# Address remainders of the fp32r row tiles, interleaved input loads, and shifted side steps in a two-block transformer kernel

## The chip, the cores and the metric

The kernel runs on one core of one Trainium2 chip. The metric is the device time of one execution in microseconds (us), and smaller is better. Engines are named as in the profile: PE (TensorE matmul), PEld (its weight loads), DVE (VectorE), ACT (ScalarE), POOL (GpSimd) and SP (SyncE), which here only issues DMAs.

## The reference

Two blocks run one after the other on x of 256 rows by 2048 features, all in fp32. What the kernel must compute, cut to its matrix products:

```
block 1: proj = rms_norm(x) @ w_in       (queries, keys, values of 3 attentions; 12 gate units)
         o1..o3 = nsa / sliding-window / moba attention, nsa also over compressed keys (cmp_w1)
         merged = sum_m sigmoid(gate_m) * (o_m @ w_branch[m]);   x += merged @ w_out
         x += relu(norm(x) @ w_mlp_in)^2 @ w_mlp_out;            x = norm(x)
block 2: proj2 = norm(x) @ w_in_2;  pool mixer and HGRN2 mixer;  x += mixed @ w_out_2
         x += cross_attention(norm(x), norm(mem)) (xattn_wq, wk, wv, wo)
         x += mixture of 16 experts (two per row), routed by norm(x);  out = norm(x)
```

## The kernel before, in words

**Weights and rows.** Up to the experts every large product is one form. SP streams weight tiles of 1 MB (two pieces of 128x1024 fp32) into the ring `RAW` of 8 pieces (`stream_load`, L199 to L218; the wait at L208 is for a free place, the plan is `make_plan`, L2165). `split` (L249 to L259) turns a piece into two fp32r halves: ACT copies it to `HI` (L257), DVE subtracts that from the piece into `LO` (L259); HI and LO have four places. `Stage.gemm` (L274) takes pieces in order. One piece is one **block**: 2 slices of the contraction x 2 halves of the rows x the three products of L301 (xh·wh), L302 (xh·wl) and L303 (xl·wh), so 12 matmuls of 128x512. The rows x are the stationary operand, 128 columns (512 bytes) of one slot; the weight piece is the moving operand. `split` is called three blocks ahead (`LEAD`), at the start of each block. After block j the function `hooks[j]` is called, and it writes its instructions into the queues at that point. That is how all other work is put beside the products: each engine works through its own queue in program order, so a waiting instruction holds all behind it on its engine.

**Where the rows lie.** The rows are kept as XH and XL, 32 slots of 128x256 fp32r each. Slots 0 to 15 are in the tensors XH and XL, which are allocated first (L117); slots 16 to 31 are in XH2 and XL2 (L128), allocated after the small tensors; RAW, HI, LO and WORK follow (L130 to L133). A partition holds 16,384 bytes of each of XH, XL, X, Y, then IDENT 512, SWH and SWL 1,536 each, GATE 192, GAIN 384, SMALL 2,048, FULL 4 (places are multiples of 32). From XH to XH2 this is 71,776 bytes, 140 x 512 + 96. XH2, XL2, RAW, HI and LO are 16,384 or 32,768 bytes long, so all of them, WORK, and later WIDE, XS and ROUNDED, start on the same remainder modulo 512, which is 96 above that of XH, XL, X, Y and IDENT.

**Which slots each stage reads** (`kt0` of `gemm`), in blocks: w_in 88 lower; 12 gate units 96 lower; cmp_w1 16 (upper slots, but 30 stationary columns and 256 moving); w_branch 16 lower and 32 upper; w_out 32 lower; the MLP 128 upper (first product) and 128 lower (second); w_in_2 80 upper; xattn_wkv, beside which HGRN runs, 64 lower; w_out_2 32 upper; xattn_wq 32 lower; xattn_wo 32 upper. That is 456 blocks on the lower slots, 304 on the upper and 16 small ones, 776 in all.

**PSUM.** A gemm accumulates in one pair of banks. It waits until the pair's last result was read (`ev[pair]`, L290): by `store` (L473; two ACT copies, L479, then a DMA) or by `add_to_x` (L483; a DVE add, L486).

**Side work the change touches.**
- Start (L523 to L579): four loads of x on SP (L527), then the weight stream; IDENT and GAIN on ACT. `first_T(c)` transposes chunk c of x (L325) and splits it (ACT L338, DVE L342). Chunks 0 and 1 come ahead of the first gemm, 2 and 3 in hooks 1 and 3. Blocks 2c and 2c+1 need chunk c.
- First gate unit (L693): `gate_weights` in hook 0 (ACT L666, DVE L668); `compress_in` (L632; PE L637 waits for a load of stored projections, L626) in hooks 1 and 4; `gate_logits` (48 small matmuls in two parts, which wait for L668) in hooks 3 and 5; `gate_values` in 7.
- Gate units 0 to 9 of L1011 all use pair 0. In units 0 to 7 runs one attention step each (`attend`, L860): transposes after block 0, `logits` after 1 (its DVE chain ends at L914), `exps(0)` after 3 and `exps(1)` after 4 (ACT, L916), `probs` after 5 (DVE, L941 to L956), `probs_T` after 6 (PE L965), `values` after 7 in banks 2 and 3, pair 1. `wide_load` is in hook 2.
- `project_add` (L1080), for w_out and w_out_2: four gemms on pairs 1, 0, 1, 0. What follows it starts on pair 0. Ahead of the w_out_2 one, the last store is of pair 1.
- HGRN (L1318 to L1493, twice): 32 blocks with steps in hooks. `exps_of(0)` after block 4; level n has its DVE work (L1415 `masked`, L1367 `exponents`, L1387 `factors`) in hook 6+2n and its matmuls (`products`, L1412) in hook 7+2n; the output steps are in hooks 25, 26, 27, 28 and 30.
- Routing, beside the last xattn_wo stage (L1682 to L1729): for chunks 0 to 2 `routed_T` (transposes, squares on ACT, `token_hi` on ACT) in hook 2c+2 and `chunk_router` (router matmuls, and `token_lo`, a DVE subtraction, L1680) in hook 2c+3; then the transposes and sums of chunk 3, the routing itself, and `token_lo(3)`.

**Experts** (from L1748): 192 MB of weights go into the ring WIDE of 24 pieces; SP waits for PE to free pieces (L236).

Of the kernel before, what the change touches and what calls it, by code (L numbers as in the profile page):

```python
# [100 lines left out]
def build(nc, a, out):  # L101
    ctx = ExitStack()
    with ctx:
        def sb(name, shape, dt=F32):
            return ctx.enter_context(nc.sbuf_tensor(name, shape, dt))
# [10 lines left out]

        lower = [sb(n, [P, DK, S], F32R) for n in ("XH", "XL")]  # L117
# [8 lines left out]
        FULL = sb("FULL", [P, 1], I32)  # L126
        upper_memory = ctx.enter_context(ExitStack())
# [71 lines left out]
        def stream_load(plan):  # L199

            b = 0
            for passes, tiles in plan:
                def body(it, base, n=2 * len(tiles)):
                    for k, (w, index) in enumerate(tiles):
                        first = base + 2 * k
                        slot = first % RAW_SLOTS

                        sp.wait_ge(lo_done, it * n + (first + 2))  # L208
                        src = w[bass.ds(index(it), 1)].rearrange("t p n -> p (t n)")
                        sp.dma_start(RAW[:, slot:slot + 2, :].rearrange("p s n -> p (s n)"), src).then_inc(raw_in[slot // 2], 16)  # L210
                assert 2 * len(tiles) % RAW_SLOTS == 0
                if passes == 1:
                    body(0, b)
                else:
                    with nc.Fori(0, passes, engines=[ENG.SP]) as it:
                        body(it, b)
                b += passes * 2 * len(tiles)
            assert b == experts  # L218
# [303 lines left out]

        small_load([a["w_in_gates"]], 24)  # L523
        x_in = [ctx.enter_context(nc.semaphore(f"x_in{c}")) for c in range(4)]
        for c in range(4):
            t = slice(c * 512, (c + 1) * 512)
            sp.dma_start(X[:, :, t], a["x"][0].rearrange("(h p) n -> p h n", p=P)[:, :, t]).then_inc(x_in[c], 16)  # L527
        dve.sem_inc(lo_done, RAW_SLOTS)
        pe.sem_inc(pe_done, HL_SLOTS)
        stream_load(plan[:-2])  # L530
        ld[2].inc(act.dma_start(IDENT[:, :], a["ident"]), 16)
        ld[2].inc(act.dma_start(GAIN[:, :, :].rearrange("p g k -> p (g k)"), a["gains"]), 16)
# [36 lines left out]

        for b in range(LEAD):  # L570
            if b < 2:
                first_T(b)
            split(b)
# [4 lines left out]
        hooks1 = {1: lambda: first_T(2), 3: lambda: first_T(3), 5: sums_of_input, 6: bias_table}  # L578
# [104 lines left out]
        def gate_values():  # L683
# [5 lines left out]
            for h in range(NH):  # L689
# [3 lines left out]
        s = gate_unit(0, {0: gate_weights, 1: lambda: compress_in(0), 3: lambda: gate_logits(0), 4: lambda: compress_in(1),  # L693
                          5: lambda: gate_logits(DK // 2), 7: gate_values})
# [165 lines left out]
        def attend(n):  # L860
# [142 lines left out]
            hooks = {0: [transposes], 1: [logits], 3: [lambda: exps(0)], 4: [lambda: exps(1)], 5: [probs], 6: [probs_T], 7: [values]}  # L1003
# [7 lines left out]
        for n in range(10):  # L1011
# [7 lines left out]
            if 2 <= n < 7:  # L1019
                hk.setdefault(2, [])  # L1020
                if n in (2, 4, 5, 6):
                    hk[2].append(lambda k={2: 0, 4: 1, 5: 2, 6: 3}[n]: wide_load(k))
            if finish:
                hk[0] = [finish] + hk.get(0, [])
            gate_unit(0, both(hk)).end()
# [54 lines left out]
        def project_add(kt0, ready, hooks, to, gain):  # L1080
# [9 lines left out]
            for c in range(4):  # L1090
# [3 lines left out]
                pair = (1, 0, 1, 0)[c]  # L1094
# [223 lines left out]
        for g in range(2):  # L1318
# [156 lines left out]
            for n in range(len(levels)):  # L1475
                k = 6 + 2 * n
# [5 lines left out]
            last = 7 + 2 * len(levels)  # L1482
# [199 lines left out]
        def routed_T(c):  # L1682

            rows_T_of_x(c)
            column_sums(c, squares=SQUARES)
            token_hi(c)

        def chunk_router(c):

            router_part(c)  # L1690
            token_lo(c)
# [26 lines left out]
        rows_T_of_x(3)  # L1718
        column_sums(3, squares=SQUARES)
# [564 lines left out]
```

## Time and profile before

| what | us |
|---|---|
| median of 3 runs | 2929.2 (2928.99 to 2929.81) |
| the profiled execution | 2927.93 |
| its span in the trace | 2926.4 |
| PE busy in the span | 2796.6 (96%) |
| DVE busy / ACT busy | 1468.2 / 1189.0 |
| DMA, MB moved | 672.70, mean 230 GB/s |

The profile gives each group of instructions by line. In a timeline row the columns are the start in us, the duration in us, engine, line, operation, the tiles (out <- in) with shapes, and the count; a bracket gives the idle time of the engine just before and what ended it. Matmuls are pipelined, so the distance between starts, not the duration, is what a matmul takes.

### The profile page before, as it was taken

The page shows a single profiled execution, that of the slowest core. Times are in us where ns is not written, and L with a number is a line of the kernel's source. Part 1 is how long each engine was busy: PE and PEld are TensorE (multiplying, and loading weights), DVE is VectorE, ACT ScalarE, POOL GpSimd, SP SyncE. Part 2 cuts the span into 40 slices and gives each one's busy share as a digit, 9 for nine tenths or more (in the row PEclk, how much of TensorE's full clock was granted, in tenths as well). Part 3 has the DMA queues.
Part 4 walks back from the last instruction along what each step waited for, and adds up shares of the span by engine and source line. Part 5 has one row for each costly group of instructions (what it writes and reads, how often), then busy time and mean ns, then how long its engine had stood idle before and what let it go on. Part 6 is the DMA issues. An engine that isn't in the chain of part 4 may idle for free.

```text
span 2926.4 us, 33379 instructions
## 1 busy us (share of the span) xinstructions
PE 2796.6 (96%) x12846; PEld 2098.3 (72%) x12846; DVE 1468.2 (50%) x1673; ACT 1189.0 (41%) x1536; POOL 12.9 (0%) x20
## 2 busy tenths in 40 slices
PE   8999999999999999999999999999999998989896
PEld 6887877777887888888887788787888774433332
DVE  4444555546655555555555744577654463312122
ACT  4443545544344444444444644545444341000001
POOL 0000000000000000000000000000000000000000
PEclk9999999999999999999999999999999998999999
DMA  7765644556646555555555475545455448999997
GB/s 276 278 210 200 245 155 155 180 177 230 225 174 221 195 186 186 186 186 185 187 174 185 166 281 207 204 150 187 170 190 184 156 161 334 419 420 419 420 419 311
DMA packets 115648, 672.70 MB, mean 230 GB/s; under 512 B 12061, under 2 KB 17613, under 8 KB 40656
## 3 DMA queue, kind: packets, MB, share of 16 engines
q1 hardware_dynamic: 85696, 612.41, 56.8%
q10 hardware_dynamic: 27552, 46.69, 4.5%
q0 software_dynamic: 2288, 12.08, 1.2%
q8 instruction: 74, 1.21, 0.2%
q14 instruction: 38, 0.31, 0.0%
HBM read 647.51 MB, written 28.35 MB: 231 GB/s over the span
## 4 chain that ended last, share of the span: by engine, by line
PE 81%; DMA 8%; ACT 4%; DVE 4%; issue 1%; DVEq 1%; ACTq 0%; SPq 0%; PEldq 0%; PEld 0%
PE PS L301 22%; PE PS L302 22%; PE PS L303 22%; PE PS L1955 6%; DMA WIDE<-in_w_up 4%; DMA WIDE<-in_w_gate 2%; DMA WIDE<-in_w_down 2%; ACT HI L257 1%; DVE LO L259 1%; PE PS L325 1%; PE PS L1893 1%; PE PS L1412 1%; ACT Y L922 1%; PE PS L2052 1%; PE PS L896 0%
## 5 line engine op out<-in xcount | busy, mean ns | idle before, releaser
L259 DVE TENSOR_TENSOR LO<-RAW,HI 128x1024 fp32r<-128x1024 f32 x776 | 941.9, 1223 | 873.2 <-ACT HI L257 868.3
L301 PE MATMUL PS<-HI,XH 128*128 128x512 f32 (+1 forms) x3104 | 1233.4, 397 | 20.5 <-DVE LO L259 7.6
L302 PE MATMUL PS<-LO,XH 128*128 128x512 f32 (+1 forms) x3104 | 1216.5, 392 | 0.0
L303 PE MATMUL PS<-HI,XL 128*128 128x512 f32 (+1 forms) x3104 | 1214.2, 391 | 0.0
L257 ACT ACTIVATE HI<-RAW 128x1024 fp32r<-128x1024 f32 x776 | 813.4, 1058 | 851.1 <-PE PS L303 774.5
L301 PEld LDWEIGHTS PS<-HI,XH 128*128 128x128 f32 (+1 forms) x3104 | 579.2, 187 | 158.5 <-issue 12.9
L303 PEld LDWEIGHTS PS<-HI,XL 128*128 128x128 f32 (+1 forms) x3104 | 578.9, 186 | 131.2
L302 PEld LDWEIGHTS PS<-LO,XH 128*128 128x128 f32 (+1 forms) x3104 | 579.4, 187 | 129.1 <-issue 2.9
L1955 PE MATMUL PS<-WIDE,XS 128*64 128x512 f32 x1024 | 229.6, 596 | 27.7 <-DMA WIDE<-in_w_up 18.4
L1955 PEld LDWEIGHTS PS<-WIDE,XS 128*64 128x64 f32 x1024 | 75.4, 137 | 166.1 <-issue 165.7
L1955 PE MATMUL PS<-WIDE,Y 128*64 128x512 f32 x512 | 116.7, 598 | 9.3 <-ACT Y L2009 5.5
L486 DVE TENSOR_TENSOR X<-PS,X 128x1024 f32<-128x1024 f32 x88 | 107.6, 1222 | 27.8 <-PE PS L303 27.8
L1955 PEld LDWEIGHTS PS<-WIDE,Y 128*64 128x64 f32 x512 | 36.4, 136 | 75.0 <-issue 67.7
L2021 DVE SCALAR_TENSOR_TENSOR ROUNDED<-PS,SMALL,ROUNDED 128x512 fp32r<-128x512 f32 x32 | 24.0, 751 | 113.9 <-ACT ROUNDED L2020 113.9
L2020 ACT ACTIVATE ROUNDED<-PS,SMALL 128x512 fp32r<-128x512 f32 x32 | 22.0, 687 | 127.8 <-PE PS L1955 127.8
L479 ACT ACTIVATE WORK<-PS,SMALL 128x512 f32<-128x512 f32 x82 | 51.8, 683 | 40.2 <-PE PS L303 38.9
L2003 DVE TENSOR_TENSOR Y<-Y,PS 128x512 f32<-128x512 f32 x8 | 5.5, 686 | 116.0 <-PE PS L1955 116.0
L2009 ACT ACTIVATE Y<-PS 128x512 f32<-128x512 f32 x8 | 4.8, 597 | 133.2 <-PE PS L2007 133.2
L1937 ACT ACTIVATE ROUNDED<-PS 128x256 fp32r<-128x256 f32 x8 | 3.1, 383 | 136.2 <-PE PS L1932 136.2
L332 ACT ACTIVATE XH<-PS 128x512 fp32r<-128x512 f32 x60 | 32.7, 594 | 60.1 <-PE PS L325 60.1
L334 DVE TENSOR_TENSOR XL<-PS,XH 128x512 fp32r<-128x512 f32 x60 | 38.7, 686 | 31.9 <-ACT XH L332 31.9
L1998 DVE TENSOR_TENSOR Y<-Y,PS 128x512 f32<-128x512 f32 x8 | 5.5, 687 | 94.8 <-ACT Y L1996 94.8
(348 smaller groups left out, 1357.0 us busy)
## 6 DMA issues: line engine op xcount, KB each, us to landing
RAW<-in_w_in SPq DMA_DIRECT2D x132, 1024.0 KB, 4.9
RAW<-in_w_mlp_in SPq DMA_DIRECT2D x64, 1024.0 KB, 4.8
RAW<-in_w_mlp_out SPq DMA_DIRECT2D x64, 1024.0 KB, 4.8
WIDE<-in_w_gate SPq DMA_DIRECT2D x64, 1024.0 KB, 23.6
WIDE<-in_w_up SPq DMA_DIRECT2D x64, 1024.0 KB, 19.7
WIDE<-in_w_down SPq DMA_DIRECT2D x64, 1024.0 KB, 22.2
RAW<-in_w_out SPq DMA_DIRECT2D x32, 1024.0 KB, 4.9
RAW<-in_xattn_wkv SPq DMA_DIRECT2D x32, 1024.0 KB, 4.8
```

The source lines that it names most:

```text
L257: act.activation(r["hi"][:, hl, :], r["raw"](k), ACT.Copy).then_inc(hi_done, 1)
L259: dve.tensor_tensor(r["lo"][:, hl, :], r["raw"](k), r["hi"][:, hl, :].bitcast(F32), ALU.subtract).then_inc(lo_done, 1)
L301: pe.matmul(o, xh, wh, start=kt == 0, stop=False)
L302: pe.matmul(o, xh, wl, start=False, stop=False)
L303: mm = pe.matmul(o, xl, wh, start=False, stop=kt == kn - 1)
L325: mm = pe.transpose(PS[:, i, q * S + h * P:q * S + h * P + P], src[:, h, (j + q) * P:(j + q + 1) * P], IDENT[:, :])
L332: hi = s_hi.inc(act.activation(dh, PS[:, i, :], ACT.Copy))
L334: lo = s_lo.inc(dve.tensor_tensor(dl, PS[:, i, :], dh.bitcast(F32), ALU.subtract))
L479: ins = act.activation(STAGE[:, slot, h * W512:(h + 1) * W512], PS[:, 2 * pair + h, :], func, scale=r[:, h:h + 1])
L486: return ev[pair].h, ev[pair].inc(dve.tensor_tensor(X[:, :, cols], pair_ap(pair), X[:, :, cols], ALU.add))
L922: act.activation(v, v, ACT.Exp, bias=NM[:, c:c + 1], accum_out=RS[:, c:c + 1])
L1955: mm = pe.matmul(PS[x * HALF:(x + 1) * HALF, bank, :], lhs(q, x), w[x][:, q, :], start=first and q == 0, stop=last and q == 3)
```

## The change

It adds two unused SBUF tensors: `shift_rows`, 96 bytes per partition, ahead of XH, and `shift_upper`, 416 bytes, between FULL and XH2. XH to Y and the small tensors move up by 96 bytes, all from XH2 on by 512. From XH to XH2 it is then 72,192 bytes, 141 x 512. The loads of x go between the first four weight tiles on SP. Hooks, pairs and the place of `token_lo` change as in the diff.

```diff
+        sb("shift_rows", [P, 24])
         lower = [sb(n, [P, DK, S], F32R) for n in ("XH", "XL")]
...
         FULL = sb("FULL", [P, 1], I32)
+        sb("shift_upper", [P, 104])
...
-        def stream_load(plan):
+        def stream_load(plan, beside):
...
                         slot = first % RAW_SLOTS
+                        if isinstance(first, int) and first < RAW_SLOTS:
+                            beside(k)
...
+        ld[2].inc(act.dma_start(IDENT[:, :], a["ident"]), 16)
+        ld[2].inc(act.dma_start(GAIN[:, :, :].rearrange("p g k -> p (g k)"), a["gains"]), 16)
         small_load([a["w_in_gates"]], 24)
...
-        for c in range(4):
+        dve.sem_inc(lo_done, RAW_SLOTS)
+        pe.sem_inc(pe_done, HL_SLOTS)
+        def input_rows(c):
             t = slice(c * 512, (c + 1) * 512)
             sp.dma_start(X[:, :, t], a["x"][0].rearrange("(h p) n -> p h n", p=P)[:, :, t]).then_inc(x_in[c], 16)
-        dve.sem_inc(lo_done, RAW_SLOTS)
-        pe.sem_inc(pe_done, HL_SLOTS)
-        stream_load(plan[:-2])
-        ld[2].inc(act.dma_start(IDENT[:, :], a["ident"]), 16)
-        ld[2].inc(act.dma_start(GAIN[:, :, :].rearrange("p g k -> p (g k)"), a["gains"]), 16)
+        stream_load(plan[:-2], input_rows)
...
+        first_T(0)
         for b in range(LEAD):
-            if b < 2:
-                first_T(b)
             split(b)
...
-        hooks1 = {1: lambda: first_T(2), 3: lambda: first_T(3), 5: sums_of_input, 6: bias_table}
+        hooks1 = {0: lambda: first_T(1), 2: lambda: first_T(2), 4: lambda: first_T(3), 5: sums_of_input, 6: bias_table}
...
-        s = gate_unit(0, {0: gate_weights, 1: lambda: compress_in(0), 3: lambda: gate_logits(0), 4: lambda: compress_in(1),
-                          5: lambda: gate_logits(DK // 2), 7: gate_values})
+        s = gate_unit(0, {0: gate_weights, 1: lambda: gate_logits(0), 2: lambda: gate_logits(DK // 2), 3: lambda: compress_in(0),
+                          4: gate_values, 5: lambda: compress_in(1)})
...
-            hooks = {0: [transposes], 1: [logits], 3: [lambda: exps(0)], 4: [lambda: exps(1)], 5: [probs], 6: [probs_T], 7: [values]}
+            hooks = {0: [transposes], 1: [logits], 2: [lambda: exps(0)], 3: [lambda: exps(1)], 4: [probs], 6: [probs_T], 7: [values]}
...
-                    hk[2].append(lambda k={2: 0, 4: 1, 5: 2, 6: 3}[n]: wide_load(k))
+                    hk[2].insert(0, lambda k={2: 0, 4: 1, 5: 2, 6: 3}[n]: wide_load(k))
...
-            gate_unit(0, both(hk)).end()
+            gate_unit(n // 9, both(hk)).end()
...
-                pair = (1, 0, 1, 0)[c]
+                pair = c % 2
...
-                k = 6 + 2 * n
+                k = 7 + 2 * n
...
-            last = 7 + 2 * len(levels)
+            last = 8 + 2 * len(levels)
...
             rows_T_of_x(c)
+            if c:
+                token_lo(c - 1)
             column_sums(c, squares=SQUARES)
...
             router_part(c)
-            token_lo(c)
...
         rows_T_of_x(3)
+        token_lo(2)
         column_sums(3, squares=SQUARES)
```

## Rows read from the trace of the kernel before

**Rows 1.** The page: busy time by engine, and the group of one DVE line.

```profile
PE 2796.6 (96%) x12846; PEld 2098.3 (72%) x12846; DVE 1468.2 (50%) x1673; ACT 1189.0 (41%) x1536; POOL 12.9 (0%) x20
...
L259 DVE TENSOR_TENSOR LO<-RAW,HI 128x1024 fp32r<-128x1024 f32 x776 | 941.9, 1223 | 873.2 <-ACT HI L257 868.3
```

**Rows 2.** Windows view: stretch, length, busy (count) by engine, PE clock, DMA share, GB/s.

```profile
2440.00:2450.00 10.00, 9.48 (x51) 6.24 (x51) 3.32 (x8) 1.67 (x2) 0.00 (x0) 0.88 0.31 125
...
2600.00:2900.00 300.00, 263.01 (x1225) 106.96 (x1222) 61.98 (x107) 24.28 (x48) 0.00 (x0) 1.00 1.01 420
```

**Rows 3.** PE's waits: who waited for whom, us in total, times, longest.

```profile
PE PS L965 <- DVE Y L956: 10.3, 8, 2.5
...
PE PS L1412 <- DVE Y L1394: 8.3, 4, 3.3
...
PE PS L301 <- ACT WORK L479: 5.7, 4, 1.4
...
PE PS L301 <- DVE X L486: 2.8, 2, 1.4
```

**Rows 4.** PE's timeline on lower slots (w_in): first and last of 85 starts.

```profile
60.16 0.40 PE L303 MATMUL PS<-HI,XL 128*128 128x512 f32 x1
...
79.76 0.40 PE L303 MATMUL PS<-HI,XL 128*128 128x512 f32 x1
```

**Rows 5.** PE's timeline on upper slots (w_in_2): first and last of 88 starts.

```profile
1700.20 0.39 PE L303 MATMUL PS<-HI,XL 128*128 128x512 f32 x1
...
1719.92 0.39 PE L303 MATMUL PS<-HI,XL 128*128 128x512 f32 x1
```

**Rows 6.** PE's timeline in the experts: 64 stationary columns, from XS and from Y.

```profile
2456.82 3.65 PE L1955 MATMUL PS<-WIDE,XS 128*64 128x512 f32 x16
...
2464.55 13.95 PE L1955 MATMUL PS<-WIDE,XS 128*64 128x512 f32 x64
...
2493.52 3.65 PE L1955 MATMUL PS<-WIDE,Y 128*64 128x512 f32 x16
```

**Rows 7.** Timeline of the start, all engines.

```profile
9.28 1.57 ACT L338 ACTIVATE XH<-PS,GAIN 128x256 fp32r<-128x256 f32 x4
...
14.44 1.06 ACT L257 ACTIVATE HI<-RAW 128x1024 fp32r<-128x1024 f32 x1 [3.59 <-DMA RAW<-in_w_in]
...
16.80 0.80 PE L301 MATMUL PS<-HI,XH 128*128 128x512 f32 x1 [3.58 <-DVE LO L259]
```

**Rows 8.** PE's timeline: second stage's start, first stop on a pair.

```profile
46.28 0.50 PE L301 MATMUL PS<-HI,XH 128*128 128x512 f32 x1 [1.36 <-ACT WORK L479]
```

**Rows 9.** Timeline of the first gate unit, all engines.

```profile
280.76 0.55 DVE L668 TENSOR_TENSOR SWL<-WORK,SWH 128x384 fp32r<-128x384 f32 x1
...
280.98 1.12 PE L637 MATMUL PS<-IDENT,Y 128*128 128x128 f32 x4 [4.82 <-DMA Y<-proj]
```

**Rows 10.** DVE's timeline in attention step 5.

```profile
537.55 0.16 DVE L914 TENSOR_SCALAR SMALL<-SMALL 128x8 f32<-128x8 f32 x1
...
544.59 1.23 DVE L259 TENSOR_TENSOR LO<-RAW,HI 128x1024 fp32r<-128x1024 f32 x1 [2.06 <-ACT HI L257]
...
547.11 1.22 DVE L956 TENSOR_TENSOR Y<-Y,SMALL 128x1024 f32<-128x1024 f32 x1
```

**Rows 11.** PE's timeline in HGRN's first pass: its stops.

```profile
1894.35 2.05 PE L1412 MATMUL PS<-Y 128*128 128x128 f32 x16 [3.31 <-DVE Y L1394]
...
1902.83 2.05 PE L1412 MATMUL PS<-Y 128*128 128x128 f32 x16 [0.83 <-DVE Y L1394]
...
1978.73 1.09 PE L325 MATMUL PS<-IDENT,WORK 128*128 128x128 f32 x8 [0.71 <-DVEq L1463]
```

**Rows 12.** Timeline of the routing: PE and DVE.

```profile
2406.08 1.09 PE L325 MATMUL PS<-IDENT,X 128*128 128x128 f32 x8 [2.18 <-DVE X L486]
...
2419.01 1.23 DVE L1680 TENSOR_TENSOR XL<-X,XH 128x1024 fp32r<-128x1024 f32 x1 [2.45 <-ACT XH L1674]
...
2421.42 1.51 PE L325 MATMUL PS<-IDENT,X 128*128 128x128 f32 x8 [2.28 <-DVE X L486]
```

## The prediction

> **What bounds the kernel now.** I read the page first: PE is busy for 96% of the span and DVE for half of it [rows 1], so up to the experts PE's own pace and its stops make the time. The windows come next, to see where that ends. In the experts DMA is busy throughout (share 1.01, 420 GB/s), while just before them its share is 0.31 [rows 2]: SP waits for PE to free the first pieces. So the experts, 201 MB at that rate or 480 us, go by DMA, but they begin when PE gets there, and what PE gains before that moves the end one for one. What it gains inside the experts is hidden by DMA.
>
> Third, PE's timeline, for the distance between starts. On lower slots 84 distances take 19.60 us, 0.2333 us each [rows 4]; on upper slots 87 take 19.72, 0.2267 each [rows 5]. The lines, shapes, HI and LO are the same, so the slot alone differs: 6.7 ns, or 2.9%. Fourth, PE's waits: some 27 us of stops in four groups that the change touches, the largest on DVE's probabilities [rows 3].
>
> **The remainder.** 456 blocks x 12 = 5472 matmuls read lower slots, and 304 x 12 = 3648 upper ones. Today HI, LO and the upper slots share a remainder, and the lower ones start 96 bytes below it; afterwards all are alike, as the upper ones are today. The trace has no lower slot at that remainder, so the cost is bounded: nothing gained, or all of 5472 x 6.67 ns = **36.5 us**. I take all. The reason: a slot's second half lies 512 bytes after its first, XL 16,384 after XH, LO as far after HI, and none of these steps shows in the distances, so the address matters, if at all, modulo 512; the other explanation, that the tensor lies far away, has to skip all these steps and act only between two tensors. Against it: with 64 stationary columns, 16 matmuls from Y, which is off the remainder, take 3.65 us as 16 from XS, which is on it [rows 6]. But there the distance is (13.95 - 3.65) / 48 = 0.215, so the load, half as long, may be no limit. Two rules of the Trainium skill speak against this part. "TensorE: Matmul & The Clock Gate", section "Back-to-back issue gap", lets the distance depend on the moving columns alone. "SBUF — State Buffer", section "Specifications (TRN2)", counts in lines of 16 bytes, of which 96 is a multiple. By either, this term would be 0; rows 4 against 5 differ all the same, and the rule is the first rival below.
>
> What becomes of the faster pace where PE waits for a chain of ACT and DVE is subtracted in each part. DVE, ACT and DMA operations keep their number and shape. The longest DVE one takes 1.22 us of a block of 12 x 0.2333 = 2.8 [rows 1, 4], so the split keeps up at 2.72.
>
> **The start.** Four loads of x (2 MB) stand ahead of the first weights. ACT has split chunk 0 at 9.28 + 1.57 = 10.85 and then waits for the weights until 14.44; PE's products begin at 16.80 [rows 7]. Afterwards 0.5 MB of x stand ahead of the 1 MB tile, half of what lands before it today, so it is there before 10.85, and all moves by 3.6. But chunk 1's eight transposes used to lie in that gap. Now they stand after block 0 in PE's way: 1.09 us for eight [rows 12], double that at the 1.2 GHz level. Net **-2.6 us**, between 0 and -3.6. The later x loads are needed two blocks apart, 5.6 us, against 1.5 MB; SP's queue issues the same eight DMAs.
>
> **First gate unit.** PE stops 4.82 us before `compress_in` for a load and goes on at 280.98 [rows 9]. The move takes this wait out of the way, since the load lands long before hook 3. But `gate_logits` now comes in hook 1, and it needs L668, which ends at 280.76 + 0.55 = 281.31 [rows 9], because ACT issues seven DMAs before the split and the gate weights. So another wait takes its place, 0.4 longer, and the two blocks ahead of it end 0.16 earlier against a fixed chain. **+0.5 us**; the bounds are -4.8 (if L668 gets done in time) and +2 (if `compress_in(1)`, now two blocks before the end, holds back the compress gemms).
>
> **Attention.** Eight stops before `probs_T`, 10.3 us [rows 3]. In step 5 the maxima are ready at 537.7 (L914), DVE splits a piece from 544.59 and the probabilities end at 548.33 (L956) [rows 10]. Now ACT waits for the maxima in hook 2 with one split (an ACT copy of 1.06 us [rows 7]) behind it instead of in front, then runs both `exps` with one split between. By my count along its queue that lets the last LO start at 543.6 instead of 544.6; the probabilities end 1.0 earlier, and PE, by now 0.4 ahead, still waits 0.4. In steps 0 and 2, `compressed_T` no longer stands between the maxima and the second exponentials, and the stop of 2.5 goes entirely. ACT's splits behind the wait have three blocks of lead, which covers them; without that cover each would cost PE 1 us. Left over I put 1.4 us, so **-8.9**; bounds -3 and -10.3. `wide_load`, put ahead of `exps(0)`, issues its three DMAs before the wait, as before.
>
> **Pairs.** PE waits for a pair to be read four times on L479, 5.7 us, and twice on L486, 2.8 [rows 3]. The first of the four, 1.36 at 46.28 [rows 8], stays. The others go: after gate units 8 and 9, around both `project_add`. Unit 9 writes banks 2 and 3, which step 7 has left by then. (5.7 - 1.36) + 2.8: **-7.1 us**. Bounds 0 and -7.1; the other pair was read a stage before.
>
> **HGRN.** Per pass PE stops 3.31 and 0.83 before `products` and 0.71 before the output transposes [rows 11]. One block more of cover is worth 2.8, but DVE's queue takes one more LO of 1.22 [rows 1] ahead of level 0's factors: 3.31 + 1.2 - 2.8 = 1.7. The second stop grows, since ACT's store of the first quarter now waits behind level 1's exponential: about 1.2. So 4.1 becomes 2.9. The chain is DVE's, and PE arrives 0.8 earlier with its faster blocks: 3.7. The output chain keeps its distance of blocks, which are 0.4 shorter in sum: 0.71 becomes 1.1. Per pass -0.4 and +0.4: **0**; bounds -3 and +2.
>
> **Routing.** PE stops 2.18 and 2.28 for L486, both times behind a `token_lo` (L1680, 1.23 us) that stands before it on DVE [rows 12]. The first loses 1.1. The second `token_lo` also waited for ACT until 2419.01, so that stop goes entirely, -2.3. In its new place the subtraction delays the last column sums by 1.2; I take them to have 0.5 of room beside the router's products (an estimate, no row here), so 0.7 comes back. **-2.7 us**; bounds 0 and -4. This chain is PE's start of the experts, so it counts in full.
>
> **The sum.** 36.5 + 2.6 - 0.5 + 8.9 + 7.1 + 0 + 2.7 = **57.3 us**. Against the profiled execution, 2927.9 (its span is 2926.4), that gives 2870.6. It stands 1.3 below the median of 2929.2; on the median, **2871.9**.
>
> **Rivals.** (1) Place, not remainder, sets the 6.7 ns. For it: rows 6 show no effect of the remainder, and the skill's rules above. Then the other terms alone remain: 2929.2 - 20.8 = **2908.4**, somewhat less since the faster pace no longer eats into gains. Chance 0.08. (2) The stops only move: a wait for the maxima at the head of ACT's queue delays splits until PE waits for LO, as in the gate unit one wait replaces another. For it: ACT and DVE are in order, and HGRN's chain is DVE's own. Against: three blocks of lead. The pace alone: 2929.2 - 36.5 = **2892.7**. Chance 0.05. (3) Slower: 512 bytes up is a worse place, and each of the 9120 matmuls loses one more such step of 6.7 ns. That costs 60.8 against 20.8 gained: **2969.2**; it decides from 2.3 ns on. Only the fact that the cause of the step is unseen speaks for it. Chance 0.02.
>
> **How the numbers follow.** The forecast has 0.85. Its own terms, with the bounds that can coincide, give -11 (the gate wait gone, no wait left in attention, HGRN at its best) and +14 (half of attention, start and routing missing, HGRN slower): 2861 to 2886. That holds some 0.83, and the other cases stay outside. Within 0.2% (5.9 us, about what a measurement of this kernel tells from no change) lies almost nothing, 0.01; slower is rival 3 with a little for an unseen wait, 0.03; faster 0.96.
>
> **What would show it.** In the profile of the changed kernel: lower-slot distances of 0.2267 (0.2333 is rival 1, over 0.2333 rival 3); the first product near 13.2; PE still stopped for 5 us in the first gate unit, now at `gate_logits` behind L668; the waits on L956 near 1.4 in sum; two waits on L479 and L486 together at most; 3.7 per pass on L1412; one stop of about 1 us in the routing. More than 3 us of PE waiting for L259 would be rival 2.

## The result, and the profile after

The changed kernel takes 2880.5 us (median of 4 runs, 2876.7 to 2882.3) against 2929.4 (2929.0 to 2929.8) for the kernel before, measured beside it: ratio 0.983, 95% interval 0.981 to 0.985. That is 48.8 us less (46.8 between the two profiled executions, 2927.9 and 2881.1). The forecast was 2871.9, 57 less, with a range of 2861 to 2886. So the direction and the range held, and 9 us of the gain are missing.

The page of the changed kernel, whose profiled execution took 2881.1 us with a span of 2879.6:

```profile
PE 2761.4 (96%) x12846; PEld 2097.8 (73%) x12846; DVE 1466.3 (51%) x1673; ACT 1186.0 (41%) x1536; POOL 12.9 (0%) x20
...
L263 DVE TENSOR_TENSOR LO<-RAW,HI 128x1024 fp32r<-128x1024 f32 x776 | 940.9, 1223 | 837.0 <-ACT HI L261 832.8
L305 PE MATMUL PS<-HI,XH 128*128 128x512 f32 (+1 forms) x3104 | 1225.5, 395 | 18.6 <-DVE LO L263 10.3
```

Its lines stand 4 to 8 lower in the file than before (L259 is now L263, L301 is L305, L965 is L971, L1412 is L1418, L1955 is L1963). The DVE subtraction takes 1.22 us as in [rows 1]. The pace is what the forecast said. In PE's timeline on a lower slot, the rows that answer to [rows 4] are these, first and last of a stretch without a pause (start, duration, then the operation):

```profile
60.10 0.39 PE L307 MATMUL PS<-HI,XL 128*128 128x512 f32 x1
...
79.82 0.39 PE L307 MATMUL PS<-HI,XL 128*128 128x512 f32 x1
```

Between them lie 87 distances: 19.72 / 87 = 0.2267 us, the value of the upper slots in [rows 5]. The difference between the slots is gone.

PE's waits (who waits <- for whom: us in total, times, longest):

```profile
PE PS L305 <- DVE LO L263: 10.3, 7, 4.4
PE PS L329 <- DMA GAIN<-in_gains: 8.9, 1, 8.9
PE PS L1418 <- DVE Y L1400: 5.5, 4, 1.6
PE PS L682 <- DVE SWL L674: 5.4, 1, 5.4
PE PS L888 <- DMA XH<-proj: 3.2, 1, 3.2
PE PS L329 <- DVEq L1469: 2.2, 2, 1.1
PE PS L1735 <- ACT SMALL L1733: 2.2, 1, 2.2
PE PS L305 <- DVE XL L661: 2.0, 1, 2.0
PE PS L305 <- ACT WORK L483: 1.9, 1, 1.9
PE PS L329 <- DVE X L490: 1.1, 1, 1.1
PE PS L971 <- DVE Y L962: 0.9, 2, 0.4
```

Against [rows 3]: the 10.3 us on the probabilities are 0.9, the four stops for a pair on L479 are one, the two on L486 are gone. But these lines are longer than before or new: GAIN (8.9, was 6.8), L674 (5.4, in the place of the 4.8 for Y<-proj), the loads XH<-proj (3.2, was 1.6), XL L661 (2.0, was not there), L1733 (2.2, was 0.5) and LO L263 (10.3, was 7.6; the wait ahead of the first product is 4.4 of it, was 3.6).

### The profile page after: what moved, and what is told of

Read it like the earlier page. It is cut to its first block, busy times and chain, and to the rows that moved or that the text cites. A ratio compares the mean times of both kernels' runs of the same rounds, so it can differ in the third digit from the quotient of the medians.

```text
span 2879.6 us, 33379 instructions
## 1 busy us (share of the span) xinstructions
PE 2761.4 (96%) x12846; PEld 2097.8 (73%) x12846; DVE 1466.3 (51%) x1673; ACT 1186.0 (41%) x1536; POOL 12.9 (0%) x20
## 3 DMA queue, kind: packets, MB, share of 16 engines
q1 hardware_dynamic: 85696, 612.41, 58.5%
## 4 chain that ended last, share of the span: by engine, by line
PE 80%; DMA 8%; DVE 5%; ACT 4%; issue 1%; DVEq 1%; ACTq 1%; SPq 0%; PEldq 0%; PEld 0%
PE PS L305 22%; PE PS L307 22%; PE PS L306 22%; PE PS L1963 6%; DMA WIDE<-in_w_up 4%; DMA WIDE<-in_w_gate 2%; DMA WIDE<-in_w_down 2%; DVE LO L263 2%; PE PS L329 1%; ACT HI L261 1%; PE PS L1901 1%; PE PS L1418 1%; PE PS L2060 1%; PE PS L902 0%; PE PS L1572 0%
## 5 line engine op out<-in xcount | busy, mean ns | idle before, releaser
L263 DVE TENSOR_TENSOR LO<-RAW,HI 128x1024 fp32r<-128x1024 f32 x776 | 940.9, 1223 | 837.0 <-ACT HI L261 832.8
L305 PE MATMUL PS<-HI,XH 128*128 128x512 f32 (+1 forms) x3104 | 1225.5, 395 | 18.6 <-DVE LO L263 10.3
L306 PE MATMUL PS<-LO,XH 128*128 128x512 f32 (+1 forms) x3104 | 1203.8, 388 | 0.0
L305 PEld LDWEIGHTS PS<-HI,XH 128*128 128x128 f32 (+1 forms) x3104 | 579.2, 187 | 143.5 <-DVE LO L263 13.9
L1963 PE MATMUL PS<-WIDE,XS 128*64 128x512 f32 x1024 | 229.4, 596 | 28.1 <-DMA WIDE<-in_w_up 18.9
L1963 PEld LDWEIGHTS PS<-WIDE,XS 128*64 128x64 f32 x1024 | 75.3, 137 | 166.5 <-issue 165.9
L1963 PE MATMUL PS<-WIDE,Y 128*64 128x512 f32 x512 | 116.7, 598 | 9.3 <-ACT Y L2017 5.5
L1963 PEld LDWEIGHTS PS<-WIDE,Y 128*64 128x64 f32 x512 | 36.4, 136 | 75.1 <-issue 67.7
L483 ACT ACTIVATE WORK<-PS,SMALL 128x512 f32<-128x512 f32 x82 | 51.7, 683 | 38.2 <-PE PS L307 36.8
```

The source lines that it names most:

```text
L263: dve.tensor_tensor(r["lo"][:, hl, :], r["raw"](k), r["hi"][:, hl, :].bitcast(F32), ALU.subtract).then_inc(lo_done, 1)
L305: pe.matmul(o, xh, wh, start=kt == 0, stop=False)
L306: pe.matmul(o, xh, wl, start=False, stop=False)
L483: ins = act.activation(STAGE[:, slot, h * W512:(h + 1) * W512], PS[:, 2 * pair + h, :], func, scale=r[:, h:h + 1])
L1963: mm = pe.matmul(PS[x * HALF:(x + 1) * HALF, bank, :], lhs(q, x), w[x][:, q, :], start=first and q == 0, stop=last and q == 3)
```

## The experiments

Twelve kernels ran. The first two split the change in its two halves; the rest ask what the remainder does and where the missing 9 us went. e1, e2 and e5 ran four times and e9 five times, the others once. They ran in three sets (e1 to e4, e5 to e8, e9 to e12), each with the kernel before beside it, whose medians were 2930.1, 2930.1 and 2932.4 (2929.4 beside the changed kernel). The changed kernel was not run again, so a time set against its 2880.5 is uncertain by some 3 us; the places in the traces are the better measure.

**e1, the pads alone, and e2, the moves alone.** e1 is the kernel before with the two pads; e2 the changed one without them.

```diff
+        sb("shift_rows", [P, 24])
         lower = [sb(n, [P, DK, S], F32R) for n in ("XH", "XL")]
...
+        sb("shift_upper", [P, 104])
         upper_memory = ctx.enter_context(ExitStack())
```

> The kernel before with the two pads alone, nothing moved. Remainder theory (the distance follows the remainder modulo 512 of the split rows against HI and LO): lower-slot distances 0.2267 us as on upper slots, 5472 x 6.67 ns = 36.5 us less, of which the longer stops give a little back (about 3): 2929.2 - 34 = 2895, between 2892 and 2899. Place theory (the lower tensors are slower for where they lie): distances stay 0.2333, time 2929 within 3. Third theory (the step of 512 bytes upward costs): distances above 0.2333 and over 2940.

> The changed kernel with its two pads taken out, all moved steps kept. Remainder theory: lower-slot distances 0.2333 again, and the time 34 above the changed kernel's 2880.5: 2914, between 2910 and 2918; the moved steps alone are then worth 2929.3 - 2914 = 15 (my forecast had 20.8 for them). Place theory: the pads do nothing, 2880.5 within 3.

Measured: e1 2901.8 us (ratio to the kernel before 0.990, interval 0.989 to 0.992), 28.3 less; e2 2908.1 (0.992, 0.991 to 0.994), 22.0 less. e1's lower slots go 0.2267 apart (19.95 us for 88 distances), e2's 0.2334 (19.84 for 85). First e1, then e2:

```profile
60.00 0.39 PE L303 MATMUL PS<-HI,XL 128*128 128x512 f32 x1
...
79.95 0.39 PE L301 MATMUL PS<-HI,XH 128*128 128x512 f32 x1
...
60.07 0.40 PE L307 MATMUL PS<-HI,XL 128*128 128x512 f32 x1
...
79.91 0.39 PE L305 MATMUL PS<-HI,XH 128*128 128x512 f32 x1
```

So the pads cause the faster matmul, and place by itself is out. But they bring 28 where 34 was expected, while the moves bring more than the 15 that then remained: 22 (18.7 by the spans of the profiled executions). Since the two halves add up to 50.3 and the change has 48.8 (by the spans 44.8 and 46.8), there is little interplay.

The four traces side by side, by the start of the same PE work:

| place | before | e1, pads | e2, moves | changed |
|---|---|---|---|---|
| second stage begins (L301/L305) | 46.28 | 45.12 | 45.49 | 45.23 |
| compress gemms done (L728/L734) | 341.73 | 334.03 | 345.61 | 338.83 |
| last value product (L984/L990) | 615.37 | 607.01 | 610.33 | 600.67 |
| work ahead of HGRN (L1257/L1263) | 1810.60 | 1786.43 | 1801.60 | 1776.29 |
| HGRN over (L1552/L1558) | 2223.64 | 2197.44 | 2208.52 | 2180.49 |
| first expert product (L1955/L1963) | 2445.44 | 2419.46 | 2426.83 | 2398.41 |
| span | 2926.4 | 2900.3 | 2907.7 | 2879.6 |

Reading e2 against before, row by row, gives each moved part alone: 0.8 won at the start, then 4.7 lost by the end of the compress gemms (from 0.8 ahead to 3.9 behind), 8.9 won in attention, 4.0 up to HGRN, 6.1 up to its end, 3.5 in the routing. Sum 18.6. The experts keep it whole: 47.0 at their first product, 46.8 at the end of the span.

**e3, rows and HI alike moved: relation or remainder?** The kernel before with the first pad only: lower slots have remainder 224, HI, LO and the upper slots 320, so the lower ones still differ by 96.

```diff
+        sb("shift_rows", [P, 24])
         lower = [sb(n, [P, DK, S], F32R) for n in ("XH", "XL")]
```

> The kernel before with the first pad only (96 bytes): the lower slots now have remainder 224, HI and LO go from 224 to 320, the upper slots too, so lower slots and HI and LO still differ by 96. If only the relation of the two operands counts: lower distances 0.2333, upper 0.2267, time 2929 within 4, as before. If the remainder of the rows by themselves (128 bad, 224 good) counts: lower distances 0.2267, time near 2895, and upper slots (320) may be worse or not. If HI and LO's own remainder of 224 is what helps: both slots change.

Measured: 2928.6 us, as before. The lower slots, at the very remainder that is fast in the changed kernel, are slow (19.83 / 85 = 0.2333):

```profile
60.10 0.39 PE L301 MATMUL PS<-HI,XH 128*128 128x512 f32 x1
...
79.93 0.39 PE L302 MATMUL PS<-LO,XH 128*128 128x512 f32 x1
```

and the upper ones, at 320 like HI and LO, are at 19.95 / 88 = 0.2267. No remainder is good in itself. What counts is how the rows stand to what is streamed. In the changed kernel XH2 starts 141 x 512 bytes after XH, an odd number of 512s, and slots of both are fast with the same HI and LO, so a period of 1024 bytes is out and one of 512 fits.

**e4 and e8, other relations.** Gaps between the tensors of the kernel before put XH, XL, XH2 and XL2 at different distances from HI and LO, modulo 512.

```diff
-        lower = [sb(n, [P, DK, S], F32R) for n in ("XH", "XL")]
+        lower = [sb("XH", [P, DK, S], F32R), (sb("gap_a", [P, 8]), sb("XL", [P, DK, S], F32R))[1]]
...
+        sb("gap_b", [P, 120])
...
+        upper_memory.enter_context(nc.sbuf_tensor("gap_c", [P, 32], F32))
...
+        work_memory.enter_context(nc.sbuf_tensor("gap_d", [P, 64], F32))
```

(e8 has gaps of 56, 40, 112 and 32 elements; a pad ahead of WIDE keeps its pieces where RAW's are.)

> The kernel before with gaps between the tensors, so that four relations stand in one trace. Remainder of the rows minus that of HI and LO: XH 32, XL 64, XH2 128, XL2 256 bytes modulo 512. If the distance only asks 'equal or not': all four 0.2333, and upper slots lose 3648 x 6.67 ns = 24: time near 2953. If it grows or falls with the difference, the four differ: the two matmuls from XH (and XH2) stand on either side of the one from XL (XL2), so each relation can be read from the spacing within a block. If the relation is not what counts at all: lower 0.2333, upper 0.2267, 2929 within 4.

> As e4, four other relations in the kernel before: remainder of the rows minus that of HI and LO is 480 (XH), 192 (XL), 448 (XH2), 384 (XL2). So far: 0 gives 0.2267 us per matmul; 32 and 64 together 0.2311; 96, 128 and 256 0.2333. If the cost depends on the plain distance of the remainders, 480 and 448 (32 and 64 below) are like 32 and 64: from XH to XL about 0.2311, time near 2945. If only rows ahead of HI and LO suffer, 480 and 448 give 0.2267 or less, and one of these could be better than 0: under 2929. If all that differ are 0.2333: 2953.

Measured: 2944.9 and 2945.8 us, both slower than before, since the upper slots lost their good relation. e4 lower, then e4 upper, then e8 lower, then e8 upper:

```profile
60.15 0.39 PE L303 MATMUL PS<-HI,XL 128*128 128x512 f32 x1
...
79.80 0.39 PE L301 MATMUL PS<-HI,XH 128*128 128x512 f32 x1
...
1700.06 0.39 PE L301 MATMUL PS<-HI,XH 128*128 128x512 f32 x1
...
1719.89 0.40 PE L302 MATMUL PS<-LO,XH 128*128 128x512 f32 x1
```

```profile
60.21 0.40 PE L303 MATMUL PS<-HI,XL 128*128 128x512 f32 x1
...
79.95 0.39 PE L301 MATMUL PS<-HI,XH 128*128 128x512 f32 x1
...
1700.19 0.39 PE L302 MATMUL PS<-LO,XH 128*128 128x512 f32 x1
...
1719.84 0.40 PE L303 MATMUL PS<-HI,XL 128*128 128x512 f32 x1
```

Each of the four stretches holds 85 distances: 0.2312 for XH 32 and XL 64 apart; 0.2333 for 128 and 256; 0.2322 for 480 and 192; 0.2312 for 448 and 384. So neither "equal or not" nor the plain distance fits, and two relations share each value. The rows above give starts to 0.01 us, too coarse to read them apart within a block, but the trace holds nanoseconds. In e4's lower stretch the three distances of a triple differ: on average 229.3 ns from one product of XH to the other, 233.4 on to XL and 230.7 back to XH. Since both the matmul and the loads beside it change from one to the next, this does not give each relation a value of its own; that stays open. Of ten relations only 0 gives 0.2267, and no pair of them was better.

**e11, LO alone apart.** The changed kernel with LO 96 bytes further, HI and all rows as they were.

```diff
+        work_memory.enter_context(nc.sbuf_tensor("gap_lo", [P, 24], F32))
         LO = work_memory.enter_context(nc.sbuf_tensor("LO", [P, HL_SLOTS, BLK], F32R))
```

> The changed kernel with LO alone 96 bytes further (remainder 320; HI and all rows 224), the same for all 9120 matmuls. If the time of a matmul follows the relation of what it streams to the rows loaded beside it, only the one of three that streams LO is slow: mean distance (2 x 0.2267 + 0.2333) / 3 = 0.2289, 3040 x 6.7 ns = 20 more, near 2901. If one slow one sets the pace of all three: 0.2333, 2880.5 + 50 = 2930 or more. If LO's place does not matter: 0.2267, 2880.5 within 3.

Measured: 2910.2 us, 30 above the changed kernel, and this on both kinds of slots (here the lower, 19.88 / 86 = 0.2312):

```profile
60.03 0.40 PE L305 MATMUL PS<-HI,XH 128*128 128x512 f32 x1
...
79.91 0.39 PE L307 MATMUL PS<-HI,XL 128*128 128x512 f32 x1
```

It lies between my first two cases. The starts in nanoseconds say which distances grew: all three. In this lower stretch it is 233.3 ns from xh·wh to xh·wl (which streams LO), 230.7 on to xl·wh and 229.4 back to xh·wh, against 226.7 each in the changed kernel; in the same stretch of the kernel before it was 231, 231 and 238. So a tensor out of step also lengthens the distance between two products that do not stream it. Why is not shown. For the kernel it means that all four tensors must agree, LO too.

**e5, the first gate unit in its old order.**

```diff
-        s = gate_unit(0, {0: gate_weights, 1: lambda: gate_logits(0), 2: lambda: gate_logits(DK // 2), 3: lambda: compress_in(0),
-                          4: gate_values, 5: lambda: compress_in(1)})
+        s = gate_unit(0, {0: gate_weights, 1: lambda: compress_in(0), 3: lambda: gate_logits(0), 4: lambda: compress_in(1),
+                          5: lambda: gate_logits(DK // 2), 7: gate_values})
```

> The changed kernel with the old order of hooks in the first gate unit (compress_in in blocks 1 and 4, gate_logits in 3 and 5), all else as changed. Against the kernel before, with pads or without, the trace shows some 5 us lost between the start of this unit and the end of the two compress gemms. If the reorder is that loss: PE stops 5.7 us for the load ahead of the first compress_in as with the pads alone, the stop of 5.4 on L674 and the one of 2.0 on L661 go, and the time is 2880.5 - 5 = 2875.5 (2874 to 2878). Rival: the unit's end is set by the same late chain (seven small DMAs on ACT) in either order, and the loss is from the half clock behind a stop: 2880.5 within 1.5.

Measured: 2874.3 us (2873.3 to 2875.5; ratio to the kernel before 0.980, interval 0.979 to 0.982), 6.2 below the changed kernel. This part of the change costs time. Changed kernel, PE's timeline (in square brackets the idle time before, and who ended it):

```profile
273.94 0.41 PE L682 MATMUL PS<-XH,SWH 128*24 128x256 f32 x1 [5.38 <-DVE SWL L674]
...
301.92 0.30 PE L305 MATMUL PS<-HI,XH 128*30 128x256 f32 x1 [2.01 <-DVE XL L661]
...
319.42 0.30 PE L305 MATMUL PS<-HI,XH 128*30 128x256 f32 x1 [0.48 <-DVE LO L263]
```

and e5:

```profile
274.78 1.11 PE L643 MATMUL PS<-IDENT,Y 128*128 128x128 f32 x4 [5.27 <-DMA Y<-proj]
...
304.08 0.30 PE L305 MATMUL PS<-HI,XH 128*30 128x256 f32 x1 [0.23 <-DVE LO L263]
```

The first stop is the same in either order, 5.3 us for a chain that starts with ACT. But `compress_in(1)` in block 5 makes the compress gemms wait 2.0 for their own input (L661), and PE's clock falls behind that stop: granted 0.50, that is 1.2 GHz, between 304 and 306. When L734 is reached, e5 is 4.2 us ahead of the changed kernel, of which 0.7 are older than this unit. It wins another 2.7 beside attention step 0, where the steps are the same (e12 shows what happens there), so the order is worth some 3.5 of the 6.2.

**e10, the loads in this unit put in another order.** On top of the changed kernel, the two loads that `compress_in` needs come first on ACT, the five small ones in block 0's hook. The steps move too: `compress_in` to blocks 1 and 3, `gate_logits` to 2 and 4.

```diff
-        for w in range(2):
-            ld[4].inc(act.dma_start(POS[:, w, :], a["cmp_pos"][w]), 16)
-            ld[4].inc(act.dma_start(W2[:, w, :, :], a["cmp_w2"][0, w].rearrange("(k p) n -> p k n", p=P)), 16)
...
+        s = gate_unit(0, {0: lambda: (gate_weights(), small_loads()), 1: lambda: compress_in(0), 2: lambda: gate_logits(0), 3: lambda: (compress_in(1), dve.wait_ge(ld[0].h, ld[0].now())),
+                          4: lambda: gate_logits(DK // 2), 5: gate_values})
```

> Only the third of these mends. Theory: ACT issued seven DMAs of 0.66 us each before the split and the gate weights, with the two that PE waits for at the end; issued first they land 3.3 earlier, the stop of 5.3 ahead of compress_in shrinks to 2.0, and no other stop takes its place up to the end of the compress gemms: 2874.3 - 3.3 = 2871. Rival: the landing itself is late for another reason (the stores of the stage before must have landed first, and ACT waits for those): the stop stays near 5 and the time near 2874.

Measured: 2869.2 us in the one run, 11.3 below the changed kernel (by place, 9.2 between the start of the second stage and L734). The stop is 2.75 (expected 2.0), and no other takes its place up to the end of the compress gemms:

```profile
271.79 0.66 PE L650 MATMUL PS<-IDENT,Y 128*128 128x128 f32 x4 [2.75 <-DMA Y<-proj]
```

In the changed kernel ACT's queue had these ahead of the two loads (start, duration):

```profile
267.52 0.37 ACTq L604 DMA_DIRECT2D SMALL<-in_swa_sinks  x1
...
269.90 1.01 ACTq L632 DMA_DIRECT2D Y<-proj  x2
```

From the first small one to the two that count it is 2.4 us (0.4 to 0.5 each, not the 0.66 of my expectation), and the stop is 2.5 shorter than e5's. So 2.5 of the stop come not from the order of the steps, but from five DMA issues on ACT ahead of the two that PE waited for. The 2.75 that are left begin where the rival of the expectation has them: in e10 ACT issues the last store of the stage before at 265.15, it lands at 267.91, and the first of the two loads follows at 267.98.

**e6, GAIN ahead of x.**

```diff
-        ld[2].inc(act.dma_start(GAIN[:, :, :].rearrange("p g k -> p (g k)"), a["gains"]), 16)
...
+        ld[2].inc(sp.dma_start(GAIN[:, :, :].rearrange("p g k -> p (g k)"), a["gains"]), 16)
         stream_load(plan[:-2], input_rows)
```

> The changed kernel with the load of GAIN issued by SP ahead of x, not by ACT beside it. Theory: the first transposes waited for GAIN until 8.87 us because the first weight tile's packets stood before it. Then they begin near 5 to 6.8, the first product comes at 13.0 instead of 15.19, and the second stage begins 2 earlier (43.2): about 2878.5. Rival: the weight tile is late next (its split could then be waiting), first product no earlier than 14.5, and the gain is under 0.7.

Measured: 2875.0 us in one run. Changed kernel, then e6:

```profile
8.87 1.97 PE L329 MATMUL PS<-IDENT,X 128*128 128x128 f32 x8 [8.87 <-DMA GAIN<-in_gains]
15.19 0.79 PE L305 MATMUL PS<-HI,XH 128*128 128x512 f32 x1 [4.36 <-DVE LO L263]
...
45.23 0.50 PE L305 MATMUL PS<-HI,XH 128*128 128x512 f32 x1 [1.91 <-ACT WORK L483]
```

```profile
6.53 1.94 PE L329 MATMUL PS<-IDENT,X 128*128 128x128 f32 x8 [6.53 <-DMA X<-in_x]
12.82 0.80 PE L305 MATMUL PS<-HI,XH 128*128 128x512 f32 x1 [4.36 <-DVE LO L263]
42.46 0.50 PE L305 MATMUL PS<-HI,XH 128*128 128x512 f32 x1 [1.91 <-ACT WORK L483]
```

PE now waits for x itself, since GAIN lands at 2.81 instead of 8.82, and everything behind it moves by 2.3 to 2.8. That is the start that I had forecast (13.2). The run as a whole is 5.5 below the changed kernel, where 2 were expected: 2.6 of them come beside attention step 0, as in e5, and not from GAIN.

**e7, step 0's two loads a unit earlier**, the six others in block 5 of step 0.

```diff
-                    pe.wait_ge(a_nsa.h, 128)
+                    pe.wait_ge(a_nsa.h if n else a_nsa0.h, 96 if n else 32)
...
-        nsa_load()
+              ... 5: [lambda: nsa_load((0,))] ...
...
+                hk[5] = [lambda: nsa_load((1, 2, 3))]
```

> The changed kernel with the eight loads of keys and values taken apart: the two of attention step 0 are issued by ACT one gate unit earlier, the six others in block 5 of step 0; PE waits for its own two alone. Theory: the stop of 3.2 us ahead of the first transposes goes, and what PE loses at half clock behind it (some 2.5) goes too or shrinks: 2880.5 - 3 to - 5.5 = 2875 to 2877.5. Rival: what is late next at that place (cmp_softmax, or the transposes' own operands) takes its place, gain under 1; and a second stop may appear in step 1 if its loads then come late.

Measured: 2875.6 us in one run, 4.9 below. PE has no stop ahead of step 0's transposes at all, and no time at half clock either: the granted clock is 1.00 from 350 to 375 us.

**e12, the HGRN steps in their old blocks.**

```diff
-                k = 7 + 2 * n
+                k = 6 + 2 * n
...
-            last = 8 + 2 * len(levels)
+            last = 7 + 2 * len(levels)
```

> The changed kernel with the old blocks of the HGRN steps (k from 6, last from 7). I had forecast 0 for this part. The traces of the moves alone give 1.5 per pass of two in its favour: then PE's waits for level 0's products are 3.4 again per pass, and the time is 3 above the changed kernel's, 2883.5 (one run; the place to look is the distance from the last transposes before to the output transposes, 1.5 longer per pass). If the part is worth 0: the distance stays, with other waits.

Measured: 2881.0 us in one run, no different from the changed kernel as a whole; the trace has to be asked. PE's waits in e12, against 5.5 in the changed kernel:

```profile
PE PS L1418 <- DVE Y L1400: 7.8, 3, 3.4
```

From the transposes that begin one pass (L1341) to the ones that begin the next, the changed kernel takes 1948.60 - 1834.59 = 114.0 us and e12 1946.79 - 1831.46 = 115.3. Over both passes, from L1263 to L1558, it is 404.2 against 408.3. So the move is worth 1.3 in one pass and up to 4.1 in all; the other 2.8 are not the move's alone, since in e12's second pass the clock is at half where a group of sixteen products runs (3.78 us instead of 2.05).

Why, then, is e12 no slower? Because it had won 3.1 us before it ever came to HGRN, with the same instructions, and wins 1.1 behind it, where PE waits 1.0 for L1733 and not 2.2: their first expert products start at 2398.3 and 2398.4. Windows of the changed kernel (window, length, busy us and count of PE, PEld, DVE, ACT, POOL, then granted clock, DMA share, GB/s):

```profile
357.00:359.00 2.00, 2.00 (x9) 1.33 (x8) 0.58 (x2) 0.00 (x0) 0.00 (x0) 1.00 0.90 239
...
363.00:365.00 2.00, 2.00 (x6) 1.52 (x6) 1.70 (x7) 0.43 (x1) 0.00 (x0) 0.50 0.87 279
```

and of e12:

```profile
357.00:359.00 2.00, 2.00 (x6) 1.51 (x6) 0.23 (x1) 0.00 (x0) 0.00 (x0) 0.50 0.86 236
...
363.00:365.00 2.00, 2.00 (x11) 1.64 (x11) 1.73 (x6) 0.00 (x1) 0.00 (x0) 1.00 0.82 328
```

PE's step 0 transposes and the last value products, changed kernel, then e12:

```profile
362.29 0.69 PE L888 MATMUL PS<-IDENT,XH 128*128 128x128 f32 x2 [3.23 <-DMA XH<-proj]
...
600.67 1.02 PE L990 MATMUL PS<-Y,WORK 128*128 128x512 f32 x2
```

```profile
361.84 0.44 PE L888 MATMUL PS<-IDENT,XH 128*128 128x128 f32 x2 [1.63 <-DMA XH<-proj]
...
597.52 1.02 PE L990 MATMUL PS<-Y,WORK 128*128 128x512 f32 x2
```

The clock is at 1.2 GHz once around this stop in either: in e12 ahead of it, where the time would have been waited away anyhow, in the changed kernel behind it. There it costs 2.7: from the one row to the other it is 238.4 us in the changed kernel and 235.7 in e12. Which of the two happens differs between executions; what decides it is not shown.

**e9, four mends together**: those of e6, e10 and e7, and the first stage on the other pair of banks, so that the second need not wait for its eviction (L483, 1.9).

```diff
-        store(0, s.gemm(8, 0, 0, hooks=hooks1, ready=ready1), 0, cols_of(PROJ, 0))
+        store(1, s.gemm(8, 0, 1, hooks=hooks1, ready=ready1), 1, cols_of(PROJ, 0))
```

(`bias_table` goes from bank 3 to bank 7.)

> The changed kernel with four mends together: GAIN loaded first by SP; the first stage on the other pair of banks, so that the second stage need not wait for its eviction; in the first gate unit the two loads that compress_in needs issued first and the five small ones in block 0's hook, with compress_in in blocks 1 and 3; step 0's two loads one unit earlier. Theory: the four losses lie in series on PE and add: -2.2 (start), -1.9 (pair), -9.5 (the order, 6.2, and 3.3 of the stop ahead of compress_in), -1.6 (what is left of the stop at step 0): 2880.5 - 15.2 = 2865.3, between 2863 and 2869. Rival: the earlier PE comes, the more it waits for chains with fixed times (DMA landing, DVE), and less than half is left: over 2872.

Measured: 2863.0 us (2861.5 to 2866.3; ratio to the kernel before 0.976, interval 0.975 to 0.978). That beats both kernels, the changed one by 17.5 where 15.2 was expected (14.8 between the profiled executions; against the kernel before in its own set it is 69.4, where the changed kernel had 48.8). The stops for L483 and for step 0's loads are gone, and these two are what is left of the others:

```profile
PE PS L329 <- DMA X<-in_x: 5.9, 1, 5.9
...
PE PS L650 <- DMA Y<-proj: 3.0, 1, 3.0
```

The gains stay: at the first expert product e9 is 61.7 us ahead of the kernel before, the changed one 47.0. The sum came as expected, the parts did not: by place, start and pair gave 4.9 (4.1 expected), the gate unit 6.9 (9.5) and step 0 3.0 (1.6).

## Why the prediction was right or wrong

- **"PE's own pace and its stops make the time", and the experts begin when PE gets there**: right. The lead at their first product, 47.0, is the lead at the end, 46.8.
- **"I take all", 36.5 us for the remainder**: the mechanism was right (e1, e3), the size was off. On top of the moves the pads are worth 2426.83 - 2398.41 = 28.4 between the traces of e2 and of the changed kernel, alone 26 to 28. Each matmul in a clear stretch did gain the 6.7 ns. But only some 8780 of the 9120 follow another product of this form by 0.26 us or less; the others come behind a stop, a step beside them or at half clock. Over these 8780 the average is 0.2310 in e2 and 0.2272 in the changed kernel, 3.8 ns less, which makes 33.0 us. And PE's idle times up to the first expert product grew by 4.8, from 53.7 to 58.5. The two make up the 28.4 within 0.2. By place, the 68 blocks or so between L734 and L990 should have given 68 x 12 x 6.7 ns = 5.5 and gave 2.9 (0.7 in e1, where the old stops were still there to take it up); HGRN's 64 should have given 5.1 and gave 2.7. The term that was mis-sized is this one: all 5472 matmuls were counted in full, and of "what becomes of the faster pace where PE waits is subtracted in each part" I had subtracted 0.4 to 0.8 in a few parts, which was too little. (One reason given for it does not hold as said either: a load of 64 columns takes 0.137 us in the changed kernel's profile and one of 128 columns 0.187, so not half.) Against the Trainium skill: "TensorE: Matmul & The Clock Gate", section "Back-to-back issue gap", gives the distance by the moving columns and has no term for addresses; e1 and e3 show that with the same columns it is 0.2267 or 0.2333, by the addresses, and the measurement decides. The Trainium skill's "SBUF — State Buffer", section "Specifications (TRN2)", counts in lines of 16 bytes; 96 bytes are whole lines, and matter all the same.
- **Start, 2.6**: 0.8 in e2. The first product came 1.7 earlier, and chunk 1's transposes and a longer stop on the pair (1.7, was 1.4) took 0.9 back. The tile was there in time, as I said; the failed step is that x is all that PE waits for at first. Ahead of [rows 7] PE waited for GAIN until 6.78, and now until 8.87, with the weight tile's packets beside it. ACT's first split, at 9.28 before, moves by as much. With GAIN first (e6) the first product comes at 12.82.
- **First gate unit, 0.5 lost**: 4.7 lost in e2, some 3.5 by place in e5's comparison, both outside the bound of 2. The stop at `gate_logits` came as forecast (0.4 to 0.6 longer than the 4.82 of [rows 9]). The step that failed is the bound for `compress_in(1)`: the stop itself was 1.8 to 2.0, but 0.3 and 1.0 of waits for LO follow it in e2, and in the changed kernel 0.5 of them and a stretch at 1.2 GHz.
- **Attention, 8.9**: 8.9 in e2 (from 3.9 behind to 5.0 ahead). That the number is the same is luck. All 10.3 us of stops are gone in e2 (0.9 are left in the changed kernel, 1.4 were forecast), and the stop for step 0's loads grew from 1.6 to 3.2, since PE came there without the time at 1.2 GHz that lay ahead of it before; that time then followed behind the stop. So 10.3 was won and 1.4 given back, where I had 1.4 of stops left over. Where the slow time falls is worth 2.7 by itself (e12), and the forecast had no term for it. e7 takes the stop out.
- **Pairs, 7.1**: in e2 the five stops are gone, 4.3 ahead of HGRN and 2.9 behind, as forecast; a new one of 0.9 for LO at the merge stands against one of 1.1 that went.
- **HGRN, 0**: about 3.2 won in e2 (6.1, less the two pair stops), just past the bound of 3. The three stops per pass of [rows 11], 4.85, became 3.3 in e2 and 3.9 in the changed kernel; the forecast had 4.8. The first is 1.6 as worked out (1.7), the third 1.1 (1.1), the second 1.1 (1.2). The step that failed is "PE arrives 0.8 earlier with its faster blocks: 3.7": the first two stops stay at 2.75 with the pads. e12 puts it back and agrees, with 1.3 in one pass and at most 4.1 in all.
- **Routing, 2.7**: 3.5 in e2. PE waits 1.1 for L1733 there and 2.2 in the changed kernel, but 1.0 in e12, which has the pads too, so this is not the pads' doing alone.
- **The rivals**: place instead of remainder fell with e1 and e3; stops that only move were real in one part, the gate unit; a worse place for the 512 bytes fell with the 0.2267. The sign of rival 2, over 3 us of waits for LO, was badly set: the kernel before has 7.6 of them already. They grew by 2.7.

So 57.3 against 47.0 at the first expert product: 8.1 too much for the pace, 1.8 for the start, 4.2 for the gate unit, 0.2 for the pairs, and 4.0 too little for HGRN and the routing. Misses of both signs meet in it.

## What to carry to other kernels

Where two slots of the same shape give different distances between matmuls, compare their addresses with those of the streamed tensors, modulo 512; here 512 bytes of pads per partition were enough. A gain in PE's pace counts in full only where PE does not wait: multiply it by the blocks in clear stretches, not by all. When a step is moved, look behind its own wait for what its engine's queue delivers late, and at the first DMAs of the kernel for small ones that now move beside a big one. And compare small changes by place in the trace: two executions of the same instructions differed by 2.7 us at one stop.

## What the runs showed that I had not expected

- The distance follows the relation of four tensors: 0.2267 us with all equal, 0.2312, 0.2322 or 0.2333 with other offsets (e4, e8), and 0.2312 with only LO apart (e11), where all three distances of a triple grew though one product of three streams LO.
- A stretch at 1.2 GHz falls ahead of a stop or behind it, from one execution to the next, with the same instructions. Behind it, it costs 2.7 us, and one run can hide a part worth 3. How much of the spread between runs comes from it was not tried (the changed kernel's four runs span 5.6 us, the kernel before's 0.8 beside it, but 7.4 in the set of e5 to e8). (The Trainium skill, "TensorE: Matmul & The Clock Gate", section "What's actually happening", says of a kernel's start that the number of slow matmuls differs from run to run; here it is seen 360 us into the kernel.)
- A load of 48 KB (GAIN), issued on ACT at 1.24 us, landed at 8.82 with a tile of 1 MB issued at 1.26 on SP beside it (that landed at 8.49), and at 6.74 with the four loads of x (512 KB each) in the tile's place. Issued first of all on SP (e6) it landed at 2.81. Whether the earlier issue or the other engine does it was not tried apart.
